# Modulation weights of a two-block layer: from TensorE products to ScalarE products and GpSimd sums

## The chip, the cores and the metric

One core of a Trainium2 chip runs the whole program. The metric is the time of the device for one execution in microseconds (us), the median of 3 runs. The tensors are float32; a product of a matrix is made on TensorE from operands split into a high and a low float32r half.

## The reference, cut to what matters

A first block (attention in 12 dilated and 4 stick-breaking heads, a gated convolutional feed-forward of width 5632) runs on 256 tokens. The second block has two layers, even (pooling and convolution) and odd (a chunked linear recurrence), over 256 latent and 256 context tokens. Both of its layers are modulated by vectors that come from a small matrix product each:

```python
s_lat = jax.nn.silu(c)              # c: (1, 2048)
s_ctx = jax.nn.silu(c_ctx)          # (2048,)
for layer in range(2):
    shift, scale, gate = split(s_lat @ ada_w[layer] + ada_b[layer], 3)        # ada_w: (2, 2048, 6144)
    h = rms_norm(x, pre_g[layer]) * (1 + scale) + shift
    shift_c, scale_c, gate_c = split(s_ctx @ ada_w[layer] + ada_b[layer], 3)
    hc = rms_norm(ctx, pre_g[layer]) * (1 + scale_c) + shift_c
    ...
    x = x + gate * rms_norm(y, post_g[layer])
```

So 2 x 2048 x 6144 weights (100 MB) are multiplied with only two vectors, in float32. Of layer 1, the gate of the context is not needed.

## The kernel before, in words

**Chunks.** Every large weight matrix is streamed by SyncE in chunks of 128x1024 float32 (512 KB, line 556) into `raw`, a ring of RING = 5 slots. For each chunk ScalarE copies the high half into `whi` (line 1125), VectorE subtracts it from the chunk and gets `wlo` (line 1676), and TensorE runs three products with the halves (line 707; in the groups `up` two, one of them with twice the columns). `whi` and `wlo` have SPLIT = 4 slots, and the split of a chunk is placed AHEAD = 3 chunks before its products. In the groups ba and bb every third `wlo` is made by GpSimd (line 578).

**Order.** `Plan` lays all chunks in one line, group after group: in0 to in11, gate0 to gate7, ba/bb, out0 to out3, up0 to up43, down0 to down3, ple, pg, then of the even layer av, bx, pw, bc, bb_, bg, ag for j = 0 to 3 and ev0 to ev3, then the odd layer (q, g, v, zf, zb, o). Each engine walks this line in its own program (`Engine.chunks`, `Tensor.group`); other work of a stage is pumped in between, one piece per chunk (`pump`).

**Modulation.** The weights `ada_w` are 96 units of four 128x512 pieces (two chunks of the same ring `raw`), 24 column groups of 512 with 4 units each. `Tensor.ada` (line 732) multiplies a unit in plain float32: the stationary operand is a 128x24 window of `Sw`, which holds the two vectors, and the four pieces go to four column strips of the array (rows 0, 32, 64, 96 of a PSUM bank):

```python
r, n = 32 * (2 * i + k), 4 * u.j + 2 * i + k
rows, X = 24, m.Sw[:, n, 22 - 2 * u.at:46 - 2 * u.at]
mm = e.matmul(m.PS[6 + u.batch % 2][r:r + rows, :], X, W[:, k, :], ...)
```

The profile records each of these matmuls twice, so a unit shows as 8 records. 85 units stand between chunks of out, up, down and of the even layer, spread evenly by `spread`; 11 are `fill`: 4 before up0, 3 before av0 and 4 before q0, where TensorE waits for a normalized activation to be transposed (`turned`, line 773). The sums are copied by ScalarE (line 1137), transposed and reduced (lines 748, 1690) in three batches, the last of them at q0.

**GpSimd** has otherwise a few DMAs (`gpsimd`, lines 582 to 628): among them `bias`, `gb_c`, `PF`, the context `CX` and, for each j of the even layer, the pooling matrix `MM`; and four sums `mt1 + mt2` (line 600).

Of the kernel before, what the change touches and what calls it, by code (L numbers as in the profile page):

```python
# [14 lines left out]
T = 256  # L15
# [7 lines left out]
ADA_BATCH = ((0, 0, 12), (1, 0, 11), (1, 11, 12))  # L23
ADA_LAG, LATER = 3, 2
FILL_B, FILL_D = 4, 3
# [28 lines left out]
class Pair:  # L54
# [8 lines left out]
class Plan:  # L63


    def __init__(self):
        self.chunks, self.splits, self.by = [], [], {}
        self.sets, self.uses = 0, [0, 0]
        self.rate = self.due = 0.0
        self.units, self.limit, self.products = 0, 0, 0  # L70
        self.held, self.later, self.mains = [], [], 0
        self.pool_every = 0
        self.n_lo = {"dve": 0, "pool": 0}

    def chunk(self, src, kt, cols):
        ch = Chunk()
        ch.src, ch.kt, ch.cols, ch.i = src, kt, cols, None
        return ch

    def stream(self, ch, split=False, behind=None):  # L80

        ch.c = len(self.chunks)
        ch.slot, ch.landed = ch.c % RING, 16 * (ch.c // RING + 1)
        ch.behind = ch.c + 1 if behind is None else behind
        if split:
# [7 lines left out]
            ch.place = -1 if ch.i < 2 else max(at, old.behind if old and old.i is None else 0)  # L93
        self.chunks.append(ch)

    def group(self, name, W, c0, cols, K, N, tm=False, raw=False, wide=False, part=None, quiet=(),
              fill=0):
# [14 lines left out]
        G.chunks, G.after, G.turns, G.fill = [], [], [], []  # L112
        for j in range(G.j0, G.j1):
            rows = W[j * kt * 128:(j + 1) * kt * 128, c0:c0 + cols]
            ch = self.chunk(rows.rearrange("(k p) c -> p k c", p=128), kt, cols)
            G.chunks.append(ch)
            self.stream(ch, not raw)
            self.mains += 1
            while self.held and self.held[0][0] <= self.mains:
                for x in self.held.pop(0)[1].chunks:  # L120
                    self.stream(x, behind=x.behind)
            if fill and j == 2:
                G.fill = self.ada(fill)
                for u in G.fill:
                    for x in u.chunks:
                        self.stream(x, behind=G.chunks[0].c)
                    self.count(*u.chunks)
                self.count(*G.chunks)
            elif not fill or j > 2:
                self.count(ch)  # L130
            self.due += 0 if j in quiet else self.rate
            G.after.append(self.ada(int(self.due)))
            self.due -= int(self.due)
# [2253 lines left out]
```

## Time and profile before

| | |
|---|---|
| median of 3 runs | 3322.84 us (3322.2 to 3324.67) |
| span of the profiled execution | 3324.0 us |
| TensorE busy, mean granted clock | 3254.6 us (98%), 0.992 |
| VectorE, ScalarE, GpSimd busy | 1583.7, 1435.2, 34.9 us |
| chain that ended last | 95% on PE: line 707 87%, line 732 3% |
| DMA | 556.66 MB, mean 167 GB/s |

No time of the profiled execution other than its span is given; the span lies inside the range of the three runs. The chain that ended last follows the work back from the last instruction; the share of a line in it is what that line held on the path. Busy shares of the other engines are means over stages that differ.

### The profile page before, as it was taken

How to read it: one execution, taken by the hardware profiler on the slowest of the kernel's cores; microseconds unless marked ns; L12 is line 12 of the kernel's file. 1: busy time of each engine (PE TensorE's matmuls, PEld its weight loads, DVE VectorE, ACT ScalarE, POOL GpSimd, SP SyncE). 2: the span in 40 equal slices, each digit the busy share in tenths (PEclk: the TensorE clock that was granted, in tenths of full speed). 3: DMA queues.
4: the chain of work that ended last, by engine and by line, in shares of the span. 5: the costliest groups of instructions: out<-in, count | busy, mean ns of one | idle time of the engine just before them, and what ended most of it. 6: DMA issues, size and time to landing. Idle time of an engine off the chain costs nothing.

```text
span 3324.0 us, 44464 instructions
## 1 busy us (share of the span) xinstructions
PE 3254.6 (98%) x18722; PEld 2717.3 (82%) x18722; DVE 1583.7 (48%) x2097; ACT 1435.2 (43%) x2032; POOL 34.9 (1%) x30
## 2 busy tenths in 40 slices
PE   8999999999999999999999999999899999999998
PEld 7988888688888877777787878788788988889886
DVE  5444556566666654456322222342644455444554
ACT  5444545455555544356222121232544444444453
POOL 0000003000000000000000000000000000000000
PEclk9999999999999999999999999999999999999999
DMA  6665556766767777765455544543423333233343
GB/s 211 180 194 182 161 161 199 241 216 226 237 227 231 237 246 239 237 210 187 147 173 168 171 149 162 165 143 99 143 87 102 96 105 111 91 107 96 107 135 120
DMA packets 394086, 556.66 MB, mean 167 GB/s; under 512 B 16880, under 2 KB 239088, under 8 KB 392736
## 3 DMA queue, kind: packets, MB, share of 16 engines
q1 hardware_dynamic: 391360, 540.08, 50.7%
q0 software_dynamic: 2240, 13.04, 1.0%
q8 instruction: 148, 2.42, 0.3%
q10 hardware_dynamic: 288, 0.70, 0.1%
q14 instruction: 50, 0.41, 0.0%
HBM read 551.53 MB, written 2.23 MB: 167 GB/s over the span
## 4 chain that ended last, share of the span: by engine, by line
PE 95%; DVE 2%; ACT 1%; DMA 1%; issue 1%; SPq 0%; DVEq 0%; ACTq 0%
PE ps L707 87%; PE ps L732 3%; PE ps L920 1%; PE ps L773 1%; PE ps L938 1%; PE ps L942 1%; DVE wlo L1676 1%; PE ps L904 0%; PE ps L880 0%; DMA CX<-in_ctx 0%; ACT whi L1125 0%; PE ps L924 0%; PE ps L833 0%; DMA raw<-in_ada_w 0%; DMA H<-in_x 0%
## 5 line engine op out<-in xcount | busy, mean ns | idle before, releaser
L1676 DVE TENSOR_TENSOR wlo<-raw,whi 128x1024 fp32r<-128x1024 f32 x819 | 1003.8, 1228 | 1301.5 <-ACT whi L1125 1299.3
L1125 ACT ACTIVATE whi<-raw 128x1024 fp32r<-128x1024 f32 x824 | 866.3, 1058 | 1235.7 <-PE ps L707 1063.4
L707 PE MATMUL ps<-HCh,whi 128*128 128x512 f32 (+1 forms) x1664 | 608.1, 365 | 0.0
L707 PE MATMUL ps<-HCl,whi 128*128 128x512 f32 (+1 forms) x1664 | 595.7, 358 | 0.0
L707 PE MATMUL ps<-HCh,wlo 128*128 128x512 f32 (+1 forms) x1664 | 595.7, 358 | 0.0
L707 PE MATMUL ps<-V,whi 128*128 128x512 f32 x1408 | 499.4, 399 | 0.0
L707 PE MATMUL ps<-V,wlo 128*128 128x256 f32 x1408 | 393.6, 280 | 0.0
L707 PE MATMUL ps<-whi,HCh 128*128 128x256 f32 (+1 forms) x1152 | 375.9, 326 | 1.5 <-DVE HCl L1790 1.5
L707 PEld LDWEIGHTS ps<-HCh,whi 128*128 128x128 f32 x1664 | 316.3, 190 | 73.3 <-issue 29.5
L707 PE MATMUL ps<-wlo,HCh 128*128 128x256 f32 (+1 forms) x1152 | 367.3, 319 | 0.0
L707 PE MATMUL ps<-whi,HCl 128*128 128x256 f32 (+1 forms) x1152 | 367.1, 319 | 0.0
L707 PEld LDWEIGHTS ps<-HCl,whi 128*128 128x128 f32 x1664 | 316.0, 190 | 46.5
L707 PEld LDWEIGHTS ps<-HCh,wlo 128*128 128x128 f32 x1664 | 316.4, 190 | 43.7 <-issue 1.0
L707 PEld LDWEIGHTS ps<-V,whi 128*128 128x128 f32 x1408 | 264.4, 188 | 84.1 <-issue 15.2
L707 PEld LDWEIGHTS ps<-V,wlo 128*128 128x128 f32 x1408 | 265.6, 189 | 0.0
L707 PEld LDWEIGHTS ps<-whi,HCh 128*128 128x128 f32 x1152 | 219.5, 191 | 23.3 <-issue 8.2
L707 PEld LDWEIGHTS ps<-wlo,HCh 128*128 128x128 f32 x1152 | 219.5, 191 | 15.1
L707 PEld LDWEIGHTS ps<-whi,HCl 128*128 128x128 f32 x1152 | 219.8, 191 | 14.2
L707 PE MATMUL ps<-whi,Uh 128*128 128x512 f32 x384 | 153.4, 399 | 0.0
L707 PE MATMUL ps<-wlo,Uh 128*128 128x512 f32 x384 | 150.5, 392 | 0.0
L707 PE MATMUL ps<-whi,Ul 128*128 128x512 f32 x384 | 150.2, 391 | 0.0
L707 PE MATMUL ps<-Uh,whi 128*128 128x256 f32 x512 | 146.5, 286 | 0.0
(310 smaller groups left out, 3828.6 us busy)
## 6 DMA issues: line engine op xcount, KB each, us to landing
raw<-in_ada_w SPq DMA_DIRECT2D x192, 512.0 KB, 4.5
raw<-in_w_up SPq DMA_DIRECT2D x176, 512.0 KB, 4.6
raw<-in_w_in SPq DMA_DIRECT2D x160, 512.0 KB, 3.9
raw<-in_od_w_in SPq DMA_DIRECT2D x160, 512.0 KB, 3.5
raw<-in_ev_w_in SPq DMA_DIRECT2D x96, 512.0 KB, 5.8
raw<-in_w_down SPq DMA_DIRECT2D x88, 512.0 KB, 4.6
raw<-in_w_out SPq DMA_DIRECT2D x32, 512.0 KB, 4.3
raw<-in_w_ple_gate SPq DMA_DIRECT2D x32, 512.0 KB, 4.3
```

The lines of the kernel that those rows point to most:

```text
L707: mm = e.matmul(to, a, b, start=first and t == 0, stop=last, skip_group_check=True)
L732: mm = e.matmul(m.PS[6 + u.batch % 2][r:r + rows, :], X, W[:, k, :], start=u.first, stop=u.last, skip_group_check=True)
L773: t = e.transpose(X.bank(m, k)[:, 128 * b:128 * b + 128], src, m.ident)
L920: e.matmul(m.ds(c), m.KD[r:r + 64, h, c // 2, :], m.hV[r:r + 64, c // 2, h * 128:h * 128 + 128], start=True, stop=True, skip_group_check=True)
L938: e.matmul(PS[7][r:r + 64, k:k + 128], m.QD[:, h, c * 64:c * 64 + 64], m.ST[:, h, c, :], start=d == 0 and h == 0 and c < 2, stop=False, sk ...
L942: t = e.matmul(PS[7][r:r + 64, k:k + 128], m.SC[r:r + 64, h, c // 2, :], m.hV[r:r + 64, c // 2, h * 128:h * 128 + 128], start=False, stop= ...
L1125: e.activation(m.whi[ch.i % SPLIT][:, 0:n], m.raw[ch.slot][:, 0:n], ACT.Copy).then_inc(S("hi"), 1)
L1676: e.tensor_tensor(m.wlo[ch.i % SPLIT][:, 0:n], m.raw[ch.slot][:, 0:n], m.whi[ch.i % SPLIT][:, 0:n].bitcast(F32), ALU.subtract).then_inc(S( ...
```

## The change

The modulation weights leave the ring `raw` and TensorE's products. They come as 384 pieces of 128x512 (256 KB) in a ring `raw_ada` of their own with ADA_SLOTS = 2 slots. For each piece ScalarE multiplies by one or two values per partition (`Copy` with a scale operand), into `acc` for the first piece of a column group and else into one of two buffers `prod`; GpSimd adds `prod` to `acc`, 15 times per column group (360 additions). After the 16 pieces TensorE sums over the partitions of `acc` with a 128x24 window of `one`, which has a single column of ones: 24 such steps of one matmul per vector, 44 matmuls in all (two vectors in layer 0 and in 8 column groups of layer 1, one in the other 4). There are 704 ScalarE products.

The pieces are placed by rates per chunk: in and gate 0.6, out 0.6, up 0.4, down 0.7, even layer 1.75 (at most 2 in a chunk), elsewhere 0. That gives 93 pieces in in and gate, 19 in out, 71 in up, 61 in down and 140 in the even layer. There are no fills and no quiet chunks. The sums stand 2 chunks behind the last piece of their column group (1 chunk in the even layer). There are two batches of transposes in place of three, one in down0 and one in the even layer; none is left at q0. The attention's last product moves from PSUM bank 6 to bank 5, since banks 6 and 7 now hold the sums from the start; its scores wait for `aa_y` in place of `aa_pt`. `XG` and `XC` use bank 6 in place of 7 for every third transpose. The scratch space for DMAs that GpSimd issues shrinks from the default to 1024 bytes per partition.

```diff
-ADA_LAG, LATER = 3, 2
-FILL_B, FILL_D = 4, 3
+ADA_SLOTS, ADA_GAP = 2, 4
...
+    def modulate(self, W):
+        self.steps = [Step() for _ in range(2 * 12 * 16)]
+        for i, x in enumerate(self.steps):
+            x.i, x.n = i, i % 16
+            x.l, x.g = divmod(i // 16, 12)
+            x.slot, x.landed = i % ADA_SLOTS, 16 * (i // ADA_SLOTS + 1)
+            x.src = W[x.l][x.n * 128:(x.n + 1) * 128, x.g * 512:(x.g + 1) * 512]
+            x.vectors = 2 if x.l == 0 or x.g < 8 else 1
+            x.adds = i + 1 - (i // 16 + 1)
+        due, at, i = 0.0, 2 * RING, 0
+        for ch in self.chunks:
+            due = min(due + ch.rate, 4.0)
+            while due >= 1 and i < len(self.steps) and len(ch.muls) < 2:
+                x = self.steps[i]
+                if x.n == 0 and ch.c < at:
+                    break
+                due -= 1
+                i += 1
+                ch.muls.append(x)
+                x.c = ch.c
+                if x.n == 15:
+                    lag = 1 if ch.wide else 2
+                    at = ch.c + 2 * lag
+                    self.chunks[ch.c + lag].sums.append(x)
...
+        for x in self.steps:
+            old = RING
+            if x.i >= ADA_SLOTS:
+                ch = self.chunks[self.steps[x.i - ADA_SLOTS].c]
+                old = ch.c + RING + AHEAD + (not ch.wide)
+                held = [r.c + RING - 1 for r in self.chunks[ch.c + 1:] if r.i is None]
+                old = min([old] + held)
+            self.chunks[old].loads.append(x)
...
 def sync(m, e):
         e.dma_start(dst, ch.src).then_inc(S(f"raw{ch.slot}"), 16)
+        for x in ch.loads:
+            if x.i >= ADA_SLOTS:
+                e.wait_ge(S("ada_mul"), x.i - ADA_SLOTS + 1)
+            e.dma_start(m.raw_ada[x.slot][:, :], x.src).then_inc(S(f"raw_ada{x.slot}"), 16)
...
 class Pool(Engine):
+    def modulate(self, ch):
+        m, S, e = self.m, self.S, self.e
+        for x in ch.muls:
+            if x.n:
+                e.wait_ge(S("ada_mul"), x.i + 1)
+                if x.adds > 1:
+                    e.wait_ge(S("ada_add"), x.adds - 1)
+                e.tensor_tensor(m.acc[:, 0:x.vectors, :], m.acc[:, 0:x.vectors, :],
+                                m.prod[x.n % 2][:, 0:x.vectors, :], ALU.add).then_inc(S("ada_add"), 1)
...
 class Tensor(Engine):
+    def modulate(self, ch):
+        m, S, e = self.m, self.S, self.e
+        for x in ch.sums:
+            if x.l == x.g == 0:
                 e.wait_ge(S("bankz"), 2)
+                e.wait_ge(S("init"), 5)
+            e.wait_ge(S("ada_add"), x.adds)
+            for v in range(x.vectors):
+                r, at = 64 * (x.g % 2) + 32 * v, 23 - 2 * x.g - v
+                mm = e.matmul(m.PS[6 + x.l][r:r + 24, :], m.one[:, at:at + 24], m.acc[:, v, :],
+                              start=x.g < 2, stop=x.g >= 10, skip_group_check=True)
+            mm.then_inc(S("ada_sum"), 1)
...
 class Scalar(Engine):
+    def modulate(self, ch):
+        m, S, e = self.m, self.S, self.e
+        for x in ch.muls:
+            if x.i == 0:
+                e.wait_ge(S("c_silu"), 1)
+            e.wait_ge(S(f"raw_ada{x.slot}"), x.landed)
+            if x.n == 0:
+                dst = m.acc
+                if x.i:
+                    e.wait_ge(S("ada_sum"), x.i // 16)
+            else:
+                dst = m.prod[x.n % 2]
+                if x.i > 2:
+                    e.wait_ge(S("ada_add"), x.adds - 2 if x.n > 2 else x.adds - x.n)
+            for v in range(x.vectors):
+                a = e.activation(dst[:, v, :], m.raw_ada[x.slot][:, :], ACT.Copy,
+                                 scale=m.Sv[:, 2 * x.n + v:2 * x.n + v + 1])
+            a.then_inc(S("ada_mul"), 1)
+        for l in ch.outs:
+            e.wait_ge(S("ada_sum"), 12 * (l + 1))
+            e.activation(m.R[l][:, :], m.PS[6 + l][:, :], ACT.Copy).then_inc(S("ada_R"), 1)
```

The order on TensorE. Before, in the groups up (V is the moving activation, `raw` the modulation weights):

```order
L707 MATMUL ps<-V,whi_57 128x512
L707 MATMUL ps<-V,wlo_61 128x256
L732 MATMUL ps<-raw_51,Sw 24x512 [waits raw3,raw2]
L732 MATMUL ps<-raw_51,Sw 24x512
L732 MATMUL ps<-raw_52,Sw 24x512 x2
L707 MATMUL ps<-V,whi_54 128x512 [waits set1,lo_dve]
```

Now, in the group down0, one of the 24 places that are left:

```order
L710 MATMUL ps<-whi_56,ACl 128x512
L710 MATMUL ps<-wlo_60,ACh 128x512
L723 MATMUL ps<-acc,one 24x512 [waits ada_add]
L723 MATMUL ps<-acc,one 24x512
L710 MATMUL ps<-whi_57,ACh 128x512 [waits pr_l,lo_dve]
```

A wait for the landed weights becomes a wait for GpSimd's last addition, and 85 places between chunks become 24.

The order on ScalarE in the groups down. Before, only the copies of the high halves:

```order
L1125 ACTIVATE whi3_57<-raw_1_50 128x1024 [waits mm,raw1]
L1125 ACTIVATE whi0_54<-raw_2_51 128x1024 [waits mm,raw2]
L1125 ACTIVATE whi1_55<-raw_0_49 128x1024 [waits mm,raw0]
L1125 ACTIVATE whi2_56<-raw_1_50 128x1024 [waits mm,raw1]
L1125 ACTIVATE whi3_57<-raw_2_51 128x1024 [waits mm,raw2]
```

Now, with the products between them:

```order
L1104 ACTIVATE whi0_54<-raw_4_53 128x1024 [waits mm,raw4]
L1121 ACTIVATE prod0_79<-raw_ada0_76,S_72 128x512 [waits ada_add,raw_ada0]
L1121 ACTIVATE prod0_79<-raw_ada0_76,S_72 128x512
L1104 ACTIVATE whi1_55<-raw_0_49 128x1024 [waits mm,raw0]
L1121 ACTIVATE prod1_80<-raw_ada1_77,S_72 128x512 [waits ada_add,raw_ada1]
L1121 ACTIVATE prod1_80<-raw_ada1_77,S_72 128x512
L1104 ACTIVATE whi2_56<-raw_1_50 128x1024 [waits mm,raw1]
```

Behind each product's two waits (GpSimd's addition two pieces back, and the landing) stand the copies that TensorE needs.

The order on GpSimd around the first pooling matrix `MM`, after group av0. Before:

```order
L610 DMA gains<-GT_124 128x128 [waits gt_c]
L615 DMA MM_137<-in_poolm 128x1024 [waits mm]
L615 DMA MM_137<-in_poolm 128x1024 [waits pl_mm] x3
```

Now:

```order
L609 DMA gains<-GT_128 128x128 [waits gt_c]
L557 TENSOR_TENSOR acc_81<-acc_81,prod0_79 128x1024 [waits ada_add,ada_mul]
L557 TENSOR_TENSOR acc_81<-acc_81,prod1_80 128x1024 [waits ada_add,ada_mul]
...
L557 TENSOR_TENSOR acc_81<-acc_81,prod0_79 128x1024 [waits ada_add,ada_mul]
L617 DMA MM_141<-in_poolm 128x1024 [waits mm]
```

Seven additions, of the pieces placed in av0, now stand ahead of this DMA.

## Rows read from the trace of the kernel before

**Rows 1.** The page, its head and part 1: busy time of each engine.
```profile
span 3324.0 us, 44464 instructions
...
PE 3254.6 (98%) x18722; PEld 2717.3 (82%) x18722; DVE 1583.7 (48%) x2097; ACT 1435.2 (43%) x2032; POOL 34.9 (1%) x30
```

**Rows 2.** Line 732 (modulation matmuls): engine, operation, count, min/median/max ns; what it waited for.
```profile
L732 PE MATMUL ps<-raw,Sw x736: 590/609/1061, 564.4 to 2135.5; 128*24 128x512 f32 x184
...
L732 PE MATMUL ps<-raw,S x32: 589/592/1057, 2356.1 to 2369.8; 128*2 128x512 f32 x32
...
  DMA raw<-in_ada_w: 11.9, 3
```

**Rows 3.** Timeline of PE, group up: start us, us, engine, line, operation.
```profile
905.03 0.28 PE L707 MATMUL ps<-V,wlo 128*128 128x256 f32 x1
905.24 1.06 PE L732 MATMUL ps<-raw,Sw 128*24 128x512 f32 x8
906.23 0.50 PE L707 MATMUL ps<-V,whi 128*128 128x512 f32 x1
906.57 0.28 PE L707 MATMUL ps<-V,wlo 128*128 128x256 f32 x1
906.68 0.40 PE L707 MATMUL ps<-V,whi 128*128 128x512 f32 x1
```

**Rows 4.** Timeline of PE in the even layer; then its window (us, busy of engines, clock, DMA).
```profile
1933.51 0.39 PE L707 MATMUL ps<-HCh,wlo 128*128 128x512 f32 x1
1933.74 0.39 PE L707 MATMUL ps<-HCl,whi 128*128 128x512 f32 x1
1937.39 1.92 PE L732 MATMUL ps<-raw,Sw 128*24 128x512 f32 x8 [3.26 <-DMA raw<-in_ada_w]
...
1938.00:1943.00 5.00, 5.00 (x17) 3.02 (x10) 2.45 (x2) 2.12 (x2) 0.00 (x0) 0.50 0.74 236
```

**Rows 5.** Timeline of PE from group out3 to group up0.
```profile
655.56 1.54 PE L773 MATMUL ps<-cst,hnb 128*128 128x128 f32 x6 [0.91 <-DVE hnb L1739]
657.03 1.92 PE L732 MATMUL ps<-raw,Sw 128*24 128x512 f32 x8
```

**Rows 6.** Line 578, line 600 (GpSimd), then timelines of POOL and DVE.
```profile
L578 POOL TENSOR_TENSOR wlo<-raw,whi x5: 2372/2382/2699, 503.3 to 539.4; 128x1024 fp32r<-128x1024 f32 x5
...
L600 POOL TENSOR_TENSOR mt<-mt,mt x4: 2402/3316/3336, 518.7 to 554.0; 128x1024 f32<-128x1024 f32 x4
...
532.81 2.37 POOL L578 TENSOR_TENSOR wlo<-raw,whi 128x1024 fp32r<-128x1024 f32 x1
...
533.07 3.20 DVE L1676 TENSOR_TENSOR wlo<-raw,whi 128x1024 fp32r<-128x1024 f32 x1 [2.71 <-ACT whi L1125]
```

**Rows 7.** Windows (us; busy, count; clock; DMA; GB/s): line 1676 in in, up, down; all in up.
```profile
40.00:280.00 240.00, 104.77 (x86) 1.00 0.62 187
700.00:1180.00 480.00, 195.70 (x160) 1.00 0.71 232
1190.00:1435.00 245.00, 102.75 (x84) 1.00 0.73 242
...
700.00:1180.00 480.00, 480.00 (x2770) 395.13 (x2769) 312.13 (x441) 253.99 (x361) 0.00 (x0) 1.00 0.71 232
```

**Rows 8.** Timeline of ACT: plain copies of 128x512, then two with pointer operands.
```profile
623.67 1.08 ACT L1212 ACTIVATE Yw<-ps 128x512 f32<-128x512 f32 x2
...
907.53 0.63 ACT L1458 ACTIVATE ACh<-cv 128x512 fp32r<-128x512 f32 x1 [1.07 <-DVE cv L2096]
...
1563.50 1.02 ACT L1168 ACTIVATE HCh<-ps,M,G 128x256 fp32r<-128x256 f32 x2
```

**Rows 9.** DMA issues in the even layer, 1730 to 2130 us: KB each, median us to landing.
```profile
raw<-in_ada_w SPq DMA_DIRECT2D x59, 512.0 KB, 4.4
```

**Rows 10.** Waits of PE: us in total, times, longest; then timeline of POOL.
```profile
PE ps L822 <- DVE Sx L1863: 3.9, 3, 2.0
...
1592.51 0.55 POOL L615 DMA_DIRECT2D MM<-in_poolm  x1 [98.28 <-PE ps L707]
```

More of the change, by code:

```diff
@@ L92, in stream, with group @@
             old = self.chunks[ch.c - RING] if ch.c >= RING else None
-            ch.place = -1 if ch.i < 2 else max(at, old.behind if old and old.i is None else 0)
+            ch.place = -1 if ch.i < 2 else max(at, old.c + 1 if old and old.i is None else 0)
+        self.products += 1
+        ch.n = self.products
         self.chunks.append(ch)
-    def group(self, name, W, c0, cols, K, N, tm=False, raw=False, wide=False, part=None, quiet=(),
-              fill=0):
+        return ch
+    def group(self, name, W, c0, cols, K, N, tm=False, raw=False, wide=False, part=None):
         kt = min(K, 1024 // cols)
@@ L111, in group @@
         G.freed, G.base = G.use + 1, 2 * G.s
-        G.chunks, G.after, G.turns, G.fill = [], [], [], []
+        G.chunks = []
         for j in range(G.j0, G.j1):
             rows = W[j * kt * 128:(j + 1) * kt * 128, c0:c0 + cols]
[L115 to L133, printed above, removed]
-            for u in G.after[-1]:
-                self.count(*u.chunks)
-                for x in u.chunks:
-                    x.behind = ch.c
-                self.held.append((self.mains + LATER, u))
-            G.turns.append([b for c, b in self.later if self.mains >= c])
-            self.later = [(c, b) for c, b in self.later if c > self.mains]
+            G.chunks.append(self.stream(rows.rearrange("(k p) c -> p k c", p=128), kt, cols, not raw, N > T))
         G.done = G.chunks[-1].n
@@ L236, in schedule @@
         p.group(f"o{g}", W, g * 512, 512, NT, T, tm=True)
+    p.modulate(A["ada_w"])
     p.places = {}
-    main = {x.c for G in p.by.values() for x in G.chunks}
     for ch in p.splits:
-        while ch.place >= 0 and ch.place not in main:
-            ch.place += 1
         p.places.setdefault(ch.place, []).append(ch)
@@ L517, in chunks @@
                 self.pump()
-            self.units(G.after[j])
-            for b in G.turns[j]:
-                self.ada_turn(b)
+            self.modulate(ch)
         return G
@@ L567, with adds @@
 class Pool(Engine):
-    def ada(self, u):
-        pass
+    through = 0
+    def modulate(self, ch):
[7 more added lines that the diff above has]
+                                m.prod[x.n % 2][:, 0:x.vectors, :], ALU.add).then_inc(S("ada_add"), 1)
+    def adds(self, last):
+        end = self.plan.by[last].chunks[-1].c + 1
+        for ch in self.plan.chunks[self.through:end]:
+            self.modulate(ch)
+        self.through = end
     def splits(self, c):
```

223 lines of the change are left out of this document (80 added, 143 removed).

## The prediction

> **What bounds the kernel now.** First the page: TensorE is busy 3254.6 of 3324.0 us; no other engine passes half [rows 1]. So a microsecond taken off TensorE's queue is a microsecond of time, as long as the engines that take over the work deliver before TensorE asks. Next, line 732: 736 + 32 = 768 records, 8 to a unit, so 96 units [rows 2]. The third view is TensorE's timeline around one unit [rows 3]. There the reader is to look at starts, not durations: the next product starts 1.20 us behind the last one before the unit, where 0.11 us is usual (906.57 to 906.68). A unit costs 1.09 us, although its 8 records of 0.59 us or more would add to 4.7: four column strips run side by side. The span is within 1.2 us of the median of the runs; I add up against the span and take 1 us off at the end. A measurement of this kernel can tell 0.2% (7 us) from no change.
>
> **What leaves TensorE.**
> - 85 units between chunks: 85 x 1.09 = 92.7 us.
> - One stall. A unit waited 3.26 us for its weights in the even layer; it then took 1.92 us instead of 1.06, and the granted clock was 0.50 in the window behind it, the 1.2 GHz level [rows 4, 3]. Products there lost some 1.9 us more (3.8 us of them at half speed). 3.3 + 0.9 + 1.9 = 6 us. The rest of the 11.9 us of landing waits [rows 2] lies in fills.
> - 11 fill units: almost nothing. They stand where TensorE waits for DVE's normalized rows anyway (the transposes at 655.56 still waited 0.91 us for `hnb`) [rows 5]. Only the last of each fill, behind the first transposes (657.03, 1.92 us long), holds up work; I take 1.3 us of it. Three times: 4 us. That unit took 1.92 us as in [rows 4], so the clock was down there with the fills too; taking them out costs no clock.
>
> Together 103 us.
>
> **What TensorE gets.** 24 sums. The two matmuls of a sum go to two strips side by side, two records each, which is the depth of a unit; so I price one like a unit, 1.09 us: 26 us. Bounds: one unit's busy time, 1.06, and, should the two matmuls run one behind the other, 2 x 1.09 [rows 3]: 25 to 52 us. If all else were hidden: 3324 - 103 + 26 = **3247 us**. The order shows the 44 matmuls and no other product of these weights on TensorE, so that part does what it says.
>
> **What hides the rest, and what it costs where it doesn't.**
>
> *ScalarE.* 704 products of 128x512. Plain copies of that size take 0.54 (two in 1.08) to 0.63 us; a 128x256 copy with pointer operands takes 0.51, against some 0.3 for half a plain one, so 0.54 + 0.2 = 0.74 is my upper bound [rows 8]. I take 0.6: 422 us, on 1435 of 3324. In up ScalarE works 254 of 480 us [rows 7]; with 0.4 pieces x 1.2 us per chunk of 2.83 us it comes to some 70%. Covered. By the Trainium skill (ScalarE: Activation LUTs, What ACT_TABLE_LOAD costs) a pointer operand adds about 93 ns to 186 ns + 0.833 ns per element; back to back that is 0.61 us, and the sum would not move.
>
> *GpSimd and VectorE, together.* This is the tight place. An addition of 128x1024 takes 2.37 us undisturbed and 3.3 disturbed [rows 6]. 300 such and 60 of half size are some 780 us for an engine with 35. But the two engines exclude each other: a `wlo` that began at 533.07, with GpSimd at work from 532.81 to 535.18, took 3.20 us, where the mean is 195.7/160 = 1.22 [rows 6, 7]: it got on only when GpSimd was done. So their times add up, per chunk. The chunk on TensorE, without units: in the groups in 240/86 = 2.79 us; up 480/160 - 0.17 = 2.83; down 245/84 - 0.17 = 2.75 [rows 7] (`spread` puts 44 units on 281 chunks there: 0.157 x 1.09 = 0.17 us per chunk). Against it:
> - groups in and gate: 0.54 additions x 2.37 + 1.22 = 2.5 of 2.79;
> - up: 0.375 x 2.37 + all of DVE's 312/160 = 1.95: 2.84 of 2.83 (a little of DVE's 1.95 reads only PSUM and isn't excluded);
> - down: 0.65 x 2.37 + 1.22 = 2.76 of 2.75.
>
> That is full to the brim, though the records hold 0.1 to 0.2 us of start and end that need no lock. A split has three chunks (8 us) of lead, so single waits of 2.4 us don't reach TensorE. I allow 12 us for those that do, here and at the sums, which wait for the last addition.
>
> *Chains with no lead.* Attention goes to and fro between TensorE, VectorE and ScalarE; TensorE already waits 3.9 us for `Sx` [rows 10]. A product (1.2 us) and an addition (2.4) get into that loop in some of 12 rounds, and the scores of 8 rounds now wait for the copy of the round before (0.54 us at most each, by [rows 8]): 8 us for both, between 0 and 12 x 3.6 = 43. The residual before up0 and the transposes of av0 now have products or additions beside them, where the chunks were quiet: 3 us. `MM` is issued when av0's last product ends, at 1592.51 [rows 10]; seven additions now stand ahead of it in GpSimd's queue, and `gb_c` waits behind the last additions of up: 3 us together.
>
> *DMA.* The bytes stay the same. In the groups in the rate rises from 187 GB/s by 0.56 x 262 KB per 2.79 us = 53, to 240: up ran at 232 with the DMA engines busy 0.71 [rows 7]. Covered. All loads leave in SyncE's queue, where a wait for `ada_mul` now stands ahead of the main chunks; two slots let it stand only one piece back. What the smaller scratch space limits no row shows: between nothing and one more landing of 4.4 us [rows 9] for `MM` and for the context; I take nothing, since those loads are few.
>
> Sum: 3247 + 12 + 8 + 3 + 3 = 3273, less 1: **3272 us**.
>
> **Rivals.**
> - *All of it hidden.* Units vanish, the two engines' turns interleave: 3247. For: lead of three chunks. Against: down's 2.76 of 2.75.
> - *The sums wait.* The 16th piece is multiplied 2 chunks ahead of the sum; product 1.2, a `wlo` in the way, two additions of 2.4: 7 us of some 8. If GpSimd lags by one addition of 3.3 us at each of 24 sums, 79 us come back: 3247 + 79 = 3326, no change. For: TensorE's queue is in order, each sum blocks all. Against: lags differ by stage; single-vector groups have time.
> - *Two slots are too few in the even layer.* At 2 pieces per chunk a slot must be multiplied (1.2), its load issued (0.4) and landed (4.4 for 512 KB, so 3.5 to 4.4 for 256 KB behind a main chunk) [rows 9]: up to 6.0 us, the chunk has 24 products, 0.23 us apart [rows 4]: 5.5. ScalarE stands, and the copies behind it. 0.5 us x some 70 chunks: 35 us, on top of the 26 allowed above: 3308.
> - *The lock decides: slower.* Place: `wlo` behind GpSimd's additions in in, gate, up and down, until the splits use up their lead. If each addition holds the pair for 3.34 us (GpSimd as the disturbed L600 row) [rows 6], a chunk needs 3.02, 3.20 and 3.39 us, 0.23, 0.37 and 0.64 more than TensorE: x 160, 176 and 88 chunks = 37 + 65 + 56 = 158 us: 3405. From 77 us on it is slower than before, that is from about 0.18 us per chunk. For: one `wlo` did stand 1.98 us. Against: 3.34 already holds DVE's 1.0 us, which is counted twice so.
>
> The Trainium skill speaks for the last one: SBUF, State Buffer, Who interferes with whom, says that a VectorE instruction with two SBUF inputs and a GpSimd one that reads SBUF take turns, each for the whole of an instruction. The trace agrees (3.20 us for 1.22). By that rule each of VectorE's other two-input instructions stands in line as well. The Trainium skill (GPSIMD Engine Reference, Engine selection) would have the additions on VectorE, GpSimd being about twice as slow with two inputs; 2.37 against 1.22 us agrees.
>
> **Chances.** Forecast (3255 to 3300) 0.60; all hidden 0.12; two slots 0.10; sums wait 0.07; lock 0.11. Faster by over 0.2%: the first three and a little of the fourth, 0.84; within 0.2% the rest of the fourth, 0.05; slower 0.11. The range reaches down to the hidden case and up to where sums and slots end: 3244 to 3324, with the sums' upper price (26 us more) inside it; the lock case is left out.
>
> **What would show it.** Line 723 with 24 groups of about 1.06 us and few waits for `acc`; line 710 as much as 707 now; POOL busy 900 to 1050 us (waits for the lock are in its records); mean of `wlo` up from 1.22 to about 1.5; products on line 1121 at 0.6 us. TensorE's idle time rises from 69 us (3324.0 less 3254.6) by 25 to 45, half of it ahead of transposes and attention. I am wrong if TensorE waits for `wlo` for more than 30 us, if the waits at the sums pass 20, or if a sum costs 2 us.

## The result, and the profile after it

The changed kernel takes **3551.67 us** (median of 4 runs, 3547.46 to 3558.22) against 3322.52 for the kernel before on the same chip: a ratio of 1.0695, 95% interval 1.0679 to 1.0710 (the two medians alone divide to 1.0690). It is 229 us slower. The prediction said 3272, faster.

The head of its page, with columns as in [rows 1]:

```profile
span 3556.4 us, 44979 instructions
PE 3262.3 (92%) x18038; PEld 2751.7 (77%) x18038; DVE 1934.9 (54%) x2093; ACT 1848.0 (52%) x2735; POOL 886.0 (25%) x390
PEclk9999898999999999999999999999999999999999
```

Two things stand out against [rows 1]. TensorE was idle 69 us and is now idle 294 (3556.4 - 3262.3). And its busy time has not fallen, although 96 units (768 records) became 24 sums (88 records).

The waits that changed, TensorE's first, then ScalarE's and SyncE's queue (engine, line, waited for: us in total, times, longest):

```profile
PE ps L710 <- DVE wlo L1662: 118.6, 90, 5.5
PE ps L723 <- POOL acc L557: 43.1, 13, 9.9
PE ps L807 <- DVE Sx L1848: 32.9, 7, 8.8
...
ACT prod L1121 <- DMA raw_ada<-in_ada_w: 361.2, 140, 10.0
ACT cv L1436 <- DVE us L2093: 71.1, 22, 4.2
ACT prod L1121 <- POOL acc L557: 26.6, 19, 4.4
...
SPq L532 <- DVE wlo L1662: 2780.3, 784, 23.2
SPq L536 <- ACT prod L1121: 130.4, 75, 8.9
```

Before, no product waited for `wlo` (only weight loads did, 8.4 us in ten), and `Sx` cost 3.9 [rows 10]. Both have become large. Behind them stands a wait that had no price in the prediction's sum (a rival gave it 35 us, in the even layer alone): ScalarE waits 361 us for `raw_ada` to land. SyncE's 2780 us for `wlo` are not a loss by themselves: before, the same queue waited 2259 us for `wlo` and 512 for the units, since it always runs ahead until a slot is free.

The groups of instructions (count | busy us, mean ns | idle before, and what ended it), which answer to [rows 6, 7, 8]:

```profile
L1662 DVE TENSOR_TENSOR wlo<-raw,whi 128x1024 fp32r<-128x1024 f32 x819 | 1282.9, 1579 | 1204.8 <-ACT whi L1104 1203.7
L557 POOL TENSOR_TENSOR acc<-acc,prod 128x1024 f32<-128x1024 f32 (+1 forms) x360 | 851.2, 2364 | 1335.6 <-ACT prod L1121 1323.8
L1121 ACT ACTIVATE prod<-raw_ada,S 128x512 f32<-128x512 f32 x660 | 438.9, 715 | 388.5 <-DMA raw_ada<-in_ada_w 361.2 <-POOL acc L557 26.6
```

Where the time went, by stage. The table takes, in each trace, the time from a stage's first product on the main line (707, now 710) to the next stage's; "pieces" are the pieces of `ada_w` that are multiplied in that stage.

| stage | pieces | before | changed | all small | ScalarE's loads | small adds | one DVE instruction |
|---|---|---|---|---|---|---|---|
| in | 54 | 275.3 | 313.1 | 283.3 | 280.3 | 290.3 | 279.5 |
| gate, attention | 39 | 212.4 | 280.8 | 218.7 | 252.3 | 240.4 | 213.7 |
| out | 19 | 106.8 | 117.3 | 102.0 | 103.8 | 108.9 | 101.7 |
| up | 71 | 527.5 | 573.5 | 504.5 | 576.6 | 504.4 | 505.1 |
| down | 61 | 256.9 | 328.2 | 250.1 | 270.3 | 289.8 | 246.9 |
| even layer, up to ev0 | 140 | 616.3 | 611.7 | 572.8 | 587.9 | 574.3 | 584.9 |

The other stages agree within 11 us in all of them. The last four columns are experiments, below.

**One stretch shows both mechanisms.** The timeline of the changed kernel in down (start us, us, engine, line; SPq is SyncE's queue, whose times are those of the issue):

```profile
1502.41 1.32 ACT L1121 ACTIVATE prod<-raw_ada,S 128x512 f32<-128x512 f32 x2
1503.64 1.05 ACT L1104 ACTIVATE whi<-raw 128x1024 fp32r<-128x1024 f32 x1
1503.81 2.40 POOL L557 TENSOR_TENSOR acc<-acc,prod 128x1024 f32<-128x1024 f32 x1 [9.33 <-ACT prod L1121]
1504.72 2.58 DVE L1662 TENSOR_TENSOR wlo<-raw,whi 128x1024 fp32r<-128x1024 f32 x1 [2.18 <-ACT whi L1104]
1507.33 0.37 SPq L532 DMA_DIRECT2D raw<-in_w_down  x1
1507.74 0.94 SPq L536 DMA_DIRECT2D raw_ada<-in_ada_w  x2
...
1512.05 1.34 ACT L1121 ACTIVATE prod<-raw_ada,S 128x512 f32<-128x512 f32 x2 [7.37 <-DMA raw_ada<-in_ada_w]
1513.30 1.04 ACT L1104 ACTIVATE whi<-raw 128x1024 fp32r<-128x1024 f32 x1
1514.37 2.53 DVE L1662 TENSOR_TENSOR wlo<-raw,whi 128x1024 fp32r<-128x1024 f32 x1 [7.07 <-ACT whi L1104]
1516.93 0.38 SPq L532 DMA_DIRECT2D raw<-in_w_down  x1
1516.96 0.79 PE L710 MATMUL ps<-whi,ACh 128*128 128x512 f32 x1 [3.21 <-DVE wlo L1662]
...
1517.00:1522.00 5.00, 5.00 (x12) 3.94 (x13) 3.22 (x1) 0.43 (x1) 2.14 (x1) 0.50 0.61 184
```

The last line is a window (us, busy of PE, PEld, DVE, ACT, POOL, granted clock, DMA share, GB/s).

- *The exclusion.* A product ends, and the addition starts (1503.81) together with the next `whi` (1503.64). The `whi` takes 1.05 us, the addition 2.40. So `wlo` begins 1.5 us before the addition ends (1506.21) and ends 1.09 us behind it: 2.58 instead of 1.23 us. In the whole trace 230 of 819 `wlo` begin inside an addition; they take 2.48 us on average, none ends before its addition does, and 230 x (2.48 - 1.23) = 288 us covers the whole growth of line 1662 over the kernel with small additions (283 us). VectorE's other instructions grew too, by some 70 us in all, such as the 22 of line 2079 in up, with two inputs: from 0.69 to 1.49 us on average.
- *The loop over the two slots.* `wlo` ends at 1507.30; only then SyncE issues the main load it held back for it (1507.33), and behind that the two loads of `raw_ada` (1507.74). They land, the product starts at 1512.05, `whi` behind it in ScalarE's queue at 1513.30, `wlo` at 1514.37, and the next main load at 1516.93. One turn is 9.65 us (1504.72 to 1514.37). The three chunks of lead are worth 8.25 us (3 x 2.75). So the turn reaches TensorE: it stands 3.21 us for this `wlo`, and behind the wait its granted clock is 0.50, the 1.2 GHz level.
- *What the wait for the product in SyncE's queue did not do.* In the stages with pieces no `whi` waited for a main load (13.2 us in the whole kernel, in pg, against 171 before). So the 130 us that SyncE waited for products made no main load late.

### The profile page after: what moved, and what is told of

Read it like the earlier page. It is cut to its first block, busy times and chain, and to the rows that moved or that the text cites. A ratio compares the mean times of both kernels' runs of the same rounds, so it can differ in the third digit from the quotient of the medians.

```text
span 3556.4 us, 44979 instructions
## 1 busy us (share of the span) xinstructions
PE 3262.3 (92%) x18038; PEld 2751.7 (77%) x18038; DVE 1934.9 (54%) x2093; ACT 1848.0 (52%) x2735; POOL 886.0 (25%) x390
## 4 chain that ended last, share of the span: by engine, by line
PE 56%; DVE 16%; ACT 10%; DMA 8%; issue 5%; POOL 3%; SPq 1%; ACTq 0%; DVEq 0%; POOLq 0%
PE ps L710 51%; DVE wlo L1662 9%; DMA raw_ada<-in_ada_w 7%; ACT whi L1104 4%; ACT prod L1121 3%; POOL acc L557 3%; DVE cv L2069 1%; DVE cg L2069 1%; PE ps L903 1%; DVE cv L2079 1%; PE ps L723 1%; DVE us L2093 1%; SPq L532 1%; PE ps L758 1%; ACT acc L1121 1%
## 5 line engine op out<-in xcount | busy, mean ns | idle before, releaser
L1662 DVE TENSOR_TENSOR wlo<-raw,whi 128x1024 fp32r<-128x1024 f32 x819 | 1282.9, 1579 | 1204.8 <-ACT whi L1104 1203.7
L557 POOL TENSOR_TENSOR acc<-acc,prod 128x1024 f32<-128x1024 f32 (+1 forms) x360 | 851.2, 2364 | 1335.6 <-ACT prod L1121 1323.8
L1104 ACT ACTIVATE whi<-raw 128x1024 fp32r<-128x1024 f32 x824 | 851.0, 1052 | 595.9 <-PE ps L710 582.6
L1121 ACT ACTIVATE prod<-raw_ada,S 128x512 f32<-128x512 f32 x660 | 438.9, 715 | 388.5 <-DMA raw_ada<-in_ada_w 361.2
L710 PE MATMUL ps<-V,whi 128*128 128x512 f32 x1408 | 511.5, 406 | 43.9 <-DVE wlo L1662 43.2
L710 PE MATMUL ps<-whi,ACh 128*128 128x512 f32 x352 | 148.8, 423 | 43.3 <-DVE wlo L1662 43.3
```

Source lines behind the costliest of these rows:

```text
L557: e.tensor_tensor(m.acc[:, 0:x.vectors, :], m.acc[:, 0:x.vectors, :], m.prod[x.n % 2][:, 0:x.vectors, :], ALU.add).then_inc(S("ada_add"), 1)
L710: mm = e.matmul(to, a, b, start=first and t == 0, stop=last, skip_group_check=True)
L1104: e.activation(m.whi[ch.i % SPLIT][:, 0:n], m.raw[ch.slot][:, 0:n], ACT.Copy).then_inc(S("hi"), 1)
L1121: a = e.activation(dst[:, v, :], m.raw_ada[x.slot][:, :], ACT.Copy, scale=m.Sv[:, 2 * x.n + v:2 * x.n + v + 1])
L1662: e.tensor_tensor(m.wlo[ch.i % SPLIT][:, 0:n], m.raw[ch.slot][:, 0:n], m.whi[ch.i % SPLIT][:, 0:n].bitcast(F32), ALU.subtract).then_inc(S( ...
```

## The experiments

Two theories stood at the start. **A, the loop:** the loads of `raw_ada` stand in SyncE's queue behind loads that wait for `wlo`. **B, the exclusion:** GpSimd's additions hold DVE's two-input instructions up. **C** was a rival: ScalarE has too much to do in order. Fourteen kernels ran, on four chips whose medians for the kernel before lie between 3318.3 and 3322.5 us.

| kernel | us | against changed |
|---|---|---|
| loads of 8 columns | 3509.40 | -42 |
| additions of 8 columns | 3338.18 | -213 |
| products of 8 columns | 3466.44 | -85 |
| all three of 8 columns | 3260.80 | -291 |
| ScalarE issues the loads | 3403.87 | -148 |
| additions on DVE | 3409.32 | -142 |
| product and addition in one DVE instruction | 3267.33 | -284 |
| GpSimd copies instead of adding | 3344.08 | -208 |
| ScalarE issues the loads, additions of 8 columns | 3275.27 | -276 |
| one DVE instruction, five slots | 3263.91 | -288 |
| no pieces in gate | 3518.00 | -34 |
| ScalarE issues the loads, additions on DVE | 3376.15 | -176 |
| ScalarE issues the loads, additions in halves | 3399.39 | -152 |
| sums one chunk later | 3533.74 | -18 |

The 95% interval of each ratio is about 0.16% either way, 5 us; with the chips' own differences of up to 4 us, what is less than some 7 us between two rows is no difference.

### Taking the sizes away, one by one

```diff
-            e.dma_start(m.raw_ada[x.slot][:, :], x.src).then_inc(S(f"raw_ada{x.slot}"), 16)
+            w = 512 if x.i < ADA_SLOTS else 8
+            e.dma_start(m.raw_ada[x.slot][:, 0:w], x.src[:, 0:w]).then_inc(S(f"raw_ada{x.slot}"), 16)
```

> The changed kernel with every load into raw_ada after the first two cut to 8 of 512 columns; products, additions, sums and every wait stay. Left out: all but 8 columns of the modulation weights (the products multiply what lies in the two slots). Theory A (the ring: a piece's load stands in SyncE's queue behind main loads that wait for a wlo, whose whi stands behind the product that waits for this load; 361 us of ScalarE's waits are for raw_ada): the waits for raw_ada fall below 100 us and the stages with the long ones give back what they lost (in 38, gate 68, down 71, so most of 177 us): 3551.67 falls to 3380 to 3430. Theory B (DVE and GpSimd shut each other out of SBUF, so the additions lengthen wlo and the cast chain): loads do not matter to it, 3530 to 3550. Theory C (ScalarE has too much to do in order): 3500 to 3550, since the 704 products stay.

3509.40 us: a miss for A as I had put it, with 290 us of waits for `raw_ada` left. The view of DMA issues (KB each, median us from issue to landing) says why, the changed kernel first:

```profile
raw_ada<-in_ada_w SPq DMA_DIRECT2D x384, 256.0 KB, 4.1
```

```profile
raw_ada<-in_ada_w SPq DMA_DIRECT2D x382, 4.0 KB, 3.3
```

A load of 4 KB lands hardly sooner than one of 256. This run says that the bytes are worth 42 us and are not the main cause; about the place of the loads it says nothing.

```diff
-                e.tensor_tensor(m.acc[:, 0:x.vectors, :], m.acc[:, 0:x.vectors, :],
-                                m.prod[x.n % 2][:, 0:x.vectors, :], ALU.add).then_inc(S("ada_add"), 1)
+                e.tensor_tensor(m.acc[:, 0:x.vectors, 0:8], m.acc[:, 0:x.vectors, 0:8],
+                                m.prod[x.n % 2][:, 0:x.vectors, 0:8], ALU.add).then_inc(S("ada_add"), 1)
```

> The changed kernel with each GpSimd addition cut to 8 of 512 columns of each vector, in its place and with its waits. Left out: the adding-up of the other 504 columns. Theory A (the ring's loads): the two-slot loop stands, only up (46 us lost, where ScalarE hardly waits for raw_ada) gives back: 3500 to 3515. Theory B (the additions shut DVE out, 851 us of them): the mean wlo falls from 1.58 to about 1.23 us, the waits of TensorE for wlo from 119 us to under 60, up and most of in, gate and down come back: 3400 to 3450. Theory C (ScalarE's load): 3530 to 3550.

3338.18 us, below even B's range. `wlo` is back to the mean of [rows 7]:

```profile
L1662 DVE TENSOR_TENSOR wlo<-raw,whi 128x1024 fp32r<-128x1024 f32 x819 | 999.7, 1229 | 1338.7 <-ACT whi L1104 1336.5
```

up is at 504.4 us, the same as with everything small. In down 40 us are left, and in gate 22: something that is not the additions. Small additions also come sooner: TensorE's waits at the sums fall from 43.1 to 6.6 us. So the 213 us are the price of the additions' length, of which the exclusion is the larger part and not all.

```diff
-                a = e.activation(dst[:, v, :], m.raw_ada[x.slot][:, :], ACT.Copy,
+                w = 512 if x.i < 3 else 8
+                a = e.activation(dst[:, v, 0:w], m.raw_ada[x.slot][:, 0:w], ACT.Copy,
```

> The changed kernel with each ScalarE product cut to 8 of 512 columns (all but those of the first three pieces); loads, additions, sums and waits stay. Left out: the product of the other columns. Theory C (704 products at 0.66 to 0.72 us, some 480 us of ScalarE's time in order ahead of whi and of the gates, decide): 3400 to 3450. Theory A: the product's duration is a small part of the loop, 3510 to 3545. Theory B: 3530 to 3550.

3466.44 us: 85 us, between what C and the others said. A product lies in every turn of the stretch above, so a shorter one shortens the turn; that this is the whole of the 85 us is not shown.

> Loads, products and additions all cut to 8 of 512 columns (the first two loads and three products whole); the sums on TensorE, every wait and every place stay. Left out: nearly all of the modulation. If the three of them are all that the change costs: 3247, what the prediction had for everything hidden (the units gone, 24 sums at 1.09 us kept), and 3240 to 3270. If waits in the order of the queues or the sums' own waits cost by themselves, whatever the sizes: 3290 to 3350.

3260.80 us. So the three of them explain 291 us, and what doesn't depend on size costs 14 us beside the 3247 that the prediction had for everything hidden.

### The two causes apart

```diff
 # sync: only the first two loads of raw_ada stay there
             if x.i >= ADA_SLOTS:
-                e.wait_ge(S("ada_mul"), x.i - ADA_SLOTS + 1)
+                continue
...
 # Scalar.modulate, behind product i
             a.then_inc(S("ada_mul"), 1)
+            if x.i + ADA_SLOTS < len(self.plan.steps):
+                y = self.plan.steps[x.i + ADA_SLOTS]
+                e.wait_ge(S("ada_mul"), x.i + 1)
+                e.dma_start(m.raw_ada[y.slot][:, :], y.src).then_inc(S(f"raw_ada{y.slot}"), 16)
```

> The changed kernel with the loads of raw_ada taken out of SyncE's queue: ScalarE issues the load of piece i+2 itself, behind its product i; the rest is as it was, the whole computation stands. The runs with small sizes gave: small additions -213 us, small products -85, small loads -42, all three -291. Theory A, in what is left of it (a part of 40 to 60 us is the place of the loads in SyncE's queue, not their traffic): ScalarE's waits for raw_ada (361 us) fall below 150 and the time to 3490 to 3515. Theory E (small loads helped by less traffic): 3540 to 3560, or worse, as ScalarE pays for each issue.

3403.87 us, three times the gain expected, with the same bytes in other places. ScalarE's waits for the landing went from 361.2 to 32.4 us:

```profile
L1121 ACT ACTIVATE prod<-raw_ada,S 128x512 f32<-128x512 f32 x660 | 441.1, 712 | 79.6 <-DMA raw_ada<-in_ada_w 32.4 <-POOL acc L557 20.0 <-ACT prod L1121 16.9
```

By stage it is the mirror of the run with small additions: in comes back and down most of the way (280.3, 270.3), up does not (576.6). In up, with 0.4 pieces per chunk, ScalarE has no wait for `raw_ada` worth naming even in the changed kernel; there the additions alone cost some 70 us.

Now this edit and the small additions together:

> The changed kernel with both: ScalarE issues the loads of raw_ada, and the GpSimd additions take 8 of 512 columns. Left out: the adding-up of the other columns. So far: changed 3551.67; ScalarE's loads alone 3403.9 (-148); small additions alone 3338.2 (-213); everything small 3260.8. Theory F (two causes, the exclusion and the loop of ScalarE, SyncE and DVE over the two slots, and each makes the other longer): together they give back all but the products' own share, 3260 to 3285, which is less than the sum of the two (361 would give 3190). Theory B alone (exclusion; ScalarE's loads help only by giving DVE's splits a better time against it): no better than small additions alone, 3325 to 3345.

3275.27 us, as theory F said. The shares hang on the order in which one takes them: the additions are worth 213 us with the loop in place and 129 without it, the loop 148 with the additions in place and 63 without them. Each lengthens the other's path, since `wlo` is a link of the loop.

The two runs with ScalarE's loads also give the price of whole additions with the loop gone, by stage: 0.3 us in in (280.3 less 280.0), 23 in gate and attention, 68 in up, 19 in down, 14 in the even layer. TensorE waits only 7.5 us at the sums there, so most of it is the exclusion.

> The changed kernel with GpSimd copying prod into acc instead of adding it (one input read from SBUF instead of two), same places and waits. Left out: the sum over the pieces. Theory B in its narrow form (only GpSimd's two-input reads shut DVE out): wlo mean 1.23 us, time 3340 to 3360. Theory B in its wide form (any pass of GpSimd over 128x1024 shuts out DVE's two-input instructions): wlo mean 1.4 to 1.6 by the copy's duration, time 3450 to 3550.

```diff
-                e.tensor_tensor(m.acc[:, 0:x.vectors, :], m.acc[:, 0:x.vectors, :],
-                                m.prod[x.n % 2][:, 0:x.vectors, :], ALU.add).then_inc(S("ada_add"), 1)
+                e.tensor_copy(m.acc[:, 0:x.vectors, :], m.prod[x.n % 2][:, 0:x.vectors, :]).then_inc(S("ada_add"), 1)
```

3344.08 us, as the narrow form would have it. But the trace takes that reading back. Its groups and one place of its timeline:

```profile
L557 POOL COPY acc<-prod 128x1024 f32<-128x1024 f32 (+1 forms) x360 | 375.3, 1043 | 1597.1 <-ACT prod L1120 1593.7
L1661 DVE TENSOR_TENSOR wlo<-raw,whi 128x1024 fp32r<-128x1024 f32 x819 | 1006.2, 1237 | 1322.9 <-ACT whi L1103 1320.8
...
931.20 1.47 POOL L557 COPY acc<-prod 128x1024 f32<-128x1024 f32 x1 [3.44 <-ACT prod L1120]
932.12 1.63 DVE L1661 TENSOR_TENSOR wlo<-raw,whi 128x1024 fp32r<-128x1024 f32 x1 [0.35 <-ACT whi L1103]
```

A copy takes 1.04 us, a `whi` 1.05, and both start together, so 172 of the 187 `wlo` that begin inside a copy do so in its last 0.17 us. The 15 that begin earlier take 1.6 to 2.1 us and end 1.07 us behind the copy, as this one (932.67 + 1.08). One-input work of GpSimd excludes such DVE instructions as well; it was merely over in time. The run doesn't tell the two forms apart by its time, and its trace speaks for the wide one. The Trainium skill (SBUF — State Buffer, Who interferes with whom) has a VectorE instruction with two SBUF inputs contend with a GpSimd instruction that reads SBUF, and asks for no number of inputs on GpSimd's side. The 15 records agree.

On top of ScalarE's loads, the additions in halves:

> ScalarE issues the loads of raw_ada, and each GpSimd addition of 128x1024 is issued as two of 128x512; the whole computation stands. The same kernel with whole additions took 3403.87 us, and with additions of 8 columns 3275.27, so 128.6 us hang on the additions. If what costs is how long one addition holds DVE off (up to 2.4 us a time): halves let DVE in between, 3340 to 3380. If what costs is the additions' sum (850 to 900 us) taken from DVE: 3400 to 3425, with GpSimd's longer total on top.

```diff
-                e.tensor_tensor(m.acc[:, 0:x.vectors, :], m.acc[:, 0:x.vectors, :],
-                                m.prod[x.n % 2][:, 0:x.vectors, :], ALU.add).then_inc(S("ada_add"), 1)
+                for v in range(x.vectors):
+                    t = e.tensor_tensor(m.acc[:, v, :], m.acc[:, v, :], m.prod[x.n % 2][:, v, :], ALU.add)
+                t.then_inc(S("ada_add"), 1)
```

3399.39 us against 3403.87: the same, just below the second range. DVE did get in: in 105 of the 300 split additions a `wlo` that began in the first half ended 1.08 to 1.10 us behind it, before the second half was over. But then that second half took 2.27 us instead of 1.29, since now GpSimd stood. What one side gained the other lost: up gained 20 us, down lost 16 and the even layer 14. The sum of the two engines' work counts, not the length of one hold.

### Is it DVE's time, or the hand-over?

> The changed kernel with the 360 additions on DVE instead of GpSimd, one chunk later in its order; products, loads and sums as they were, the whole computation stands. DVE gets 360 x 1.23 us, 440 us, so it is as busy (about 2020 us) as it was made by the additions on GpSimd (1935). Theory B (what costs is the exclusion: DVE stands still up to 2.4 us whenever GpSimd holds SBUF): wlo back at 1.23 us, time 3340 to 3380. Theory D (DVE's time alone costs, whoever takes it): 3500 to 3560.

```diff
 # Vector.modulate, for the pieces of the chunks before; nothing of it on GpSimd
...
+                e.tensor_tensor(m.acc[:, 0:x.vectors, :], m.acc[:, 0:x.vectors, :],
+                                m.prod[x.n % 2][:, 0:x.vectors, :], ALU.add).then_inc(S("ada_add"), 1)
```

And the same with ScalarE issuing the loads:

> ScalarE issues the loads of raw_ada, and the 360 additions stand on DVE; the whole computation stands. With SyncE's loads the additions on DVE gave 3409.3 us, with ScalarE's loads the additions on GpSimd 3403.9. Theory F: neither the exclusion nor the loop over SyncE is left, only DVE's and ScalarE's own time: 3275 to 3310. Theory D (DVE's 407 us of additions cost by themselves, for ScalarE waits 131 us for them): 3340 to 3400.

3409.32 and 3376.15 us: neither theory's range in the first, D's in the second. `wlo` is at 1227 ns, so no exclusion is left. Two other waits came, here in the second kernel:

```profile
ACT prod L1115 <- DVE acc L1673: 136.6, 61, 4.5
PE ps L717 <- DVE acc L1673: 53.0, 10, 15.7
```

ScalarE's product waits for `prod` to be emptied by an addition in DVE's queue, with the copies to `whi` behind it, and TensorE waits at the sums.

> Product and addition in one DVE instruction (scalar_tensor_tensor on raw_ada and acc), 704 of 0.6 to 0.75 us, 420 to 530 us; nothing of it on ScalarE or GpSimd; loads in SyncE's queue and sums as they were, the whole computation stands. Theory B: 3290 to 3350, since ScalarE loses 468 us too (small products gave 85 us). Theory D: 3480 to 3560.

```diff
 # Vector.modulate; nothing of it on ScalarE or GpSimd
...
+                        t = e.scalar_tensor_tensor(m.acc[:, v, :], m.raw_ada[x.slot][:, :], s, m.acc[:, v, :],
+                                                   ALU.mult, ALU.add)
```

3267.33 us (ratio to before 0.9838, 0.9822 to 0.9854), below even B's range. DVE is busier than in any other kernel, and TensorE doesn't suffer:

```profile
PE 3173.8 (97%) x18038; PEld 2713.3 (83%) x18038; DVE 2031.5 (62%) x2797; ACT 1432.2 (44%) x2031; POOL 34.9 (1%) x30
L1662 DVE SCALAR_TENSOR_TENSOR acc<-raw_ada,S,acc 128x512 f32<-128x512 f32 x660 | 467.7, 746 | 43.1 <-DMA raw_ada<-in_ada_w 35.7
```

So D falls as "DVE's time costs": DVE gives some 470 us here, and the time stays within 7 us of everything small (the even layer alone is 12 us longer). Its 407 us of additions cost 101 us with ScalarE's loads (3376.15 against 3275.27), 34 of them in up and 67 in the even layer. ScalarE's products at full size cost 14 us at most (3275.27 against 3260.80). So neither engine's own time explains the 101 us. What does is the hand-over from ScalarE to a second engine and back, in queues that both also carry the splits; that is read from the two waits above, and no run separates it from both engines being fuller at once.

With `prod` gone, its 8 KB hold three more slots:

```diff
-ADA_SLOTS, ADA_GAP = 2, 4
+ADA_SLOTS, ADA_GAP = 5, 4
-        self.prod = [self.sb(f"prod{i}", [128, 2, 512], F32, at + 4 * i) for i in range(2)]
-        at += 8
```

> Product and addition in one DVE instruction as in the run that gave 3267.3 us, and since prod is no longer needed, five slots of raw_ada in its place, whose loads stand five pieces back in SyncE's queue; the whole computation stands. DVE waits 35.7 us for raw_ada there, in 38 waits. Theory F: these waits go, 3255 to 3265. Theory B: 3264 to 3270, since that kernel has neither an exclusion nor a wait that reaches TensorE.

3263.91 us, ratio 0.9830 (0.9816 to 0.9845): inside F's range and at the edge of B's, 3 us from the kernel with two slots, which is no difference clear of noise. The waits for `raw_ada` are gone, and they cost next to nothing. This and the kernel with two slots are the best versions, 1.6 to 1.7% ahead of the kernel before, with the whole computation.

### Two smaller questions

> The changed kernel with the rates of pieces moved: none in gate and attention (39 before), 88 instead of 71 in up and 161 instead of 140 in the even layer; the whole computation stands. If a piece costs where it stands (gate lost 62 us against everything small, for 39 pieces, 1.6 us each; up 69 for 71; even 39 for 140): gate gives back 62, the 17 pieces more in up cost 17, the 21 in even 6: 3505 to 3520. If the costs shift on to whatever stage has the pieces, at the mean of 0.76 us of all 384: 3540 to 3555.

```diff
-    p.rate = 0.6
+    p.rate = 0.0
     for g in range(8):
...
-    p.rate = 0.4
+    p.rate = 0.5
```

3518.00 us, inside the first range, but not by its terms. Gate is back at 212.4 us exactly (-68), up rose by 33 for 17 pieces more, twice what was said, and the even layer fell by 4 for 21 more, where a rise of 6 was said. In gate and in up the cost stands where the pieces do, and in up it grows faster than their number; in the even layer it did not grow.

> The changed kernel with each sum on TensorE one chunk later (3 chunks behind the last product of its column group instead of 2, in up 2 instead of 1), and the next group's pieces one chunk later too; the whole computation stands. TensorE waits 43.1 us in 13 waits for additions at the sums. If these waits cost by themselves: most go, 3510 to 3530. If they are only where TensorE happens to stand while the additions and the splits are late anyway: 3540 to 3555.

```diff
-                    at = ch.c + 2 * lag
-                    self.chunks[ch.c + lag].sums.append(x)
+                    at = ch.c + 2 * lag + 1
+                    self.chunks[ch.c + lag + 1].sums.append(x)
```

3533.74 us, just above the first range. The waits at the sums fell from 43.1 to 8.7 us, those for `wlo` rose from 118.6 to 134.1:

```profile
PE ps L710 <- DVE wlo L1662: 134.1, 93, 6.2
...
PE ps L723 <- POOL acc L557: 8.7, 5, 5.3
```

34 us of waits at the sums went and 18 us of the time: about half of them were a cost of their own. The even layer gave back 24 us and down 8, while up took 4 more. In up as in the even layer the sum stood one chunk behind the last product, not two.

## Why the prediction was wrong

**Right.** *What leaves TensorE.* 44 units on 281 chunks are 27 in up, 30 us, less 5 sums, 5.5: up should lose 24.5. With the additions small it went from 527.5 to 504.4. *The sums.* Their records take 592 ns at the least and 610 in the median, like a unit's [rows 2], and a sum that waits for nothing puts 1.06 to 1.08 us between the products around it, with one matmul or with two (1.09 said). *All hidden, 3247.* The kernel with everything small took 3260.8; of the 14 us, `in` (+8.0) and gate (+6.3) hold some 9 beyond the five sums they got, and down 4. What those are made of is open. *The product* is 0.66 us (two in 1.32), inside 0.54 to 0.74, where I took 0.6. *GpSimd's addition* of 128x1024 2.41 us in the median, *the mean of `wlo`* 1.58 where I wrote about 1.5. Two of the three signs of being wrong came: the waits for `wlo` passed 30 us and those at the sums 20. `MM` delayed TensorE by 1.8 us.

**Wrong, first step: "A split has three chunks (8 us) of lead, so single waits of 2.4 us don't reach TensorE. I allow 12 us."** TensorE waits 118.6 us for `wlo` and 43.1 at the sums. I had the exclusion, its size (2.5 of 2.79, 2.84 of 2.83, 2.76 of 2.75 us per chunk) and the growth of `wlo`, and then treated a chunk filled to the brim as one that keeps its lead. It doesn't: the lead is rebuilt only by slack. With ScalarE's loads, where the exclusion is left without the loop, whole additions cost 0.3 us in `in`, where the sum left 0.29 us per chunk, and 68 in up, where it left none; 129 in all, where I allowed 12. Nor do the waits come single: since addition and `whi` start together and `wlo` follows 1.05 us later, an addition catches the split beside it.

**Wrong, second step: "two slots let it stand only one piece back. Covered."** I looked at the bandwidth, and it was mostly covered (the small loads gave 42 us). I did not follow whom the loads stand behind: SyncE's queue stands at `wlo` most of the time (2780 us), which waits for `whi`, which stands behind the product that waits for the load. It is worth 148 us, and 63 without the exclusion. The rival "two slots are too few" had the mechanism's first link, but set it in the even layer, by the multiplying, issuing and landing of the piece alone; the even layer lost 39 us against all small, down 78 and gate 62.

**Mis-sized: attention, 8 us with 43 as its bound.** gate went up by 68.4 us. `Sx` alone took 32.9 us of TensorE's time, seven waits of up to 8.8; with small additions 13.5, so the exclusion has its part in this too. Without pieces there, all 68 came back.

**Not in the sum at all: the clock.** The kernels with everything small and with everything at size issue the same instructions on TensorE, yet it is busy 3169.1 and 3262.3 us. A third of the loss (93 of 298 us of span) is slower products, not idle time. The stretches gate and down, first with the changed kernel (window: us, PE busy, PEld, DVE, ACT, POOL, granted clock, DMA share, GB/s):

```profile
331.50:612.40 280.90, 229.35 (x990) 185.37 (x988) 154.96 (x147) 155.71 (x229) 95.61 (x40) 0.90 0.51 163
1350.60:1678.80 328.20, 271.49 (x1076) 207.64 (x1077) 187.74 (x106) 173.68 (x236) 141.60 (x59) 0.94 0.61 193
```

and with everything small:

```profile
301.60:520.40 218.80, 207.82 (x990) 170.58 (x988) 109.75 (x146) 122.81 (x230) 19.71 (x40) 1.00 0.54 162
1173.30:1423.40 250.10, 246.06 (x1078) 198.46 (x1077) 111.55 (x104) 122.07 (x234) 21.53 (x59) 1.00 0.59 189
```

The same 990 records of gate took 229 and 208 us, at a granted clock of 0.90 and 1.00 (1.00 is the 2.4 GHz level, so a part of the stretch behind TensorE's waits ran at 1.2). I had [rows 4], where one stall brought the clock to the 1.2 GHz level, and used it only for the stall that goes away.

**The rivals.** "The lock decides: slower" had the direction and half of the mechanism; its time was 3405. Its stages were in 37, up 65, down 56; measured against before, 37.9, 46.0 and 71.3, or against all small, 30, 69 and 78. That these are close is luck outside up: the exclusion without the loop is 0.3, 68 and 19, and the rest of in and down is the loop, which the rival did not have. Its price was wrong too, by the argument I held against it: it let each addition hold the pair for 3.34 us, and 257 of the 300 whole additions took under 2.9. It left out gate (68) and the even layer (39 against all small). I gave it 0.11. "The sums wait" was worth 18 us, most of it in the even layer, where the sum stands one chunk behind and not the two of the rival's sum. "All hidden" is nearly what one gets when nothing is handed over.

The Trainium skill (GPSIMD Engine Reference, Engine selection) would put the additions on VectorE. The runs agree in the direction, 3409 against 3552 us; moved there one by one they still cost more than the units on TensorE did, and only fused with the product they are nearly free.

## What to carry to other kernels

A lead of n chunks hides a late instruction only if the engine has slack to win the lead back: here 0.29 us of slack per chunk was enough in `in`, and none in up was not. When the sum of the times per chunk comes to the chunk, price the whole excess and its spread, not a few single waits. Before a small ring is called covered by bandwidth, follow its load round: what stands ahead of it in the queue that issues it, what that waits for, and whether the consumer stands ahead of that very thing in its own queue. And work taken off the engine that bounds should go where it needs no second engine: 470 us on one engine in its own order cost 3 to 7 us more than everything small, 470 us on ScalarE and 850 on GpSimd cost 290.

## What was not expected of the hardware

- A load of 4 KB (128 rows of 32 bytes) landed after 3.3 us, one of 256 KB after 4.1.
- In the changed kernel and in the one with copies, a `wlo` that begins inside a GpSimd instruction ends 1.07 to 1.22 us behind its end, mostly 1.08 behind an addition, whether it is an addition or a copy; alone it takes 1.23.
- The granted clock of gate and attention went from 1.00 to 0.90 with TensorE idle 52 of 281 us there instead of 11 of 219, and the products became 10% longer: idle time was paid for one and a half times.
- What stays open: what the 17 us between the best version (3263.91) and all of it hidden (3247) are made of. That wasn't tried.
